# Softmax heads of 128 values kept feature-side, with the probabilities normalised before their turning

## The reference

```python
def _layer_c(x, norm_g, w_in, w_out, pos):
    h = jnp.matmul(_rmsnorm(x, norm_g).astype(x.dtype), w_in)
    cq, ck, cv, z = jnp.split(h, [C_WIDTH, 2 * C_WIDTH, 3 * C_WIDTH], axis=-1)
    yc = _moba_attention(_rope(_heads(cq, C_HEADS), pos), _rope(_heads(ck, C_HEADS), pos), _heads(cv, C_HEADS))
    y = _merge(yc) * jax.nn.silu(z)
    return x + jnp.matmul(y.astype(x.dtype), w_out)
```

## Time and profile before

| | |
|---|---|
| median of 3 runs | 1805.94 us |
| the profiled execution | 1806.85 us |
| its span (first to last instruction) | 1805.0 us |
| TensorE matmuls busy | 1794.4 us, 99% |
| VectorE busy | 1207.6 us, 67% |
| ScalarE busy | 1014.4 us, 56% |
| GpSimd busy | 160.5 us, 9% |
| granted TensorE clock, mean | 0.999 of 2.4 GHz |
| transposes of `ty` (L972) | 112 |
| wide matmuls (L801 to L804) | 768 each |

### The profile page before, as it was taken

The page is one execution under the profiler, slowest core; times in us unless marked ns, Lnnn a source line. Parts: engine busy times, 40 slices in busy tenths (PEclk is TensorE's granted clock), DMA queues, the critical chain, the costliest instruction groups (busy, mean ns, idle before and its releaser), DMA issues.

```text
span 1805.0 us, 26929 instructions
## 1 busy us (share of the span) xinstructions
PE 1794.4 (99%) x10712; PEld 1620.7 (90%) x10712; DVE 1207.6 (67%) x1669; ACT 1014.4 (56%) x1614; POOL 160.5 (9%) x128
## 2 busy tenths in 40 slices
PE   9999999999999999999999999999999999999998
PEld 7999888888899999998889999888888999988887
DVE  6665655555666897697658888655565888855554
ACT  7436546665557765875553444666454344546644
POOL 0000000110011111100001111001000111100101
PEclk9999999999999999999999999999999999999999
DMA  9557555555555555445566555554555655555464
GB/s 361 200 175 223 185 181 191 180 173 189 195 185 170 169 172 174 153 166 173 190 207 203 197 182 187 193 184 166 186 190 197 202 198 175 182 188 185 165 210 139
DMA packets 96620, 340.29 MB, mean 189 GB/s; under 512 B 10880, under 2 KB 11520, under 8 KB 96368
## 3 DMA queue, kind: packets, MB, share of 16 engines
q1 hardware_dynamic: 95120, 334.44, 54.9%
q0 software_dynamic: 944, 3.61, 0.6%
q10 hardware_dynamic: 432, 0.53, 0.1%
HBM read 336.44 MB, written 2.10 MB: 188 GB/s over the span
## 4 chain that ended last, share of the span: by engine, by line
PE 98%; DMA 1%; DVE 0%; ACT 0%; SPq 0%; issue 0%; DVEq 0%; ACTq 0%
PE ACC L796 18%; PE ACC L798 18%; PE ACC L797 18%; PE ACC L804 9%; PE ACC L801 9%; PE ACC L803 5%; PE ACC L802 5%; PE ACC L809 2%; PE ACC L810 2%; PE ACC L811 2%; PE PM L919 1%; PE PM L934 1%; DMA RAW<-in_w 1%; PE PM L972 1%; PE PM L957 1%; PE PM L956 1%
## 5 line engine op out<-in xcount | busy, mean ns | idle before, releaser
L1587 DVE TENSOR_TENSOR WL<-RAW,WH 128x1024 fp32r<-128x1024 f32 (+2 forms) x632 | 792.4, 1271 | 468.6 <-ACT WH L1175 467.2
L1175 ACT ACTIVATE WH<-RAW 128x1024 fp32r<-128x1024 f32 (+3 forms) x633 | 647.2, 1039 | 411.5 <-PE ACC L798 219.1
L796 PE MATMUL ACC<-WH,XHL 128*128 128x512 f32 (+1 forms) x1044 | 395.5, 379 | 0.5 <-DVE WL L1587 0.5
L798 PE MATMUL ACC<-WH,XHL 128*128 128x512 f32 (+1 forms) x1044 | 389.0, 373 | 0.0
L797 PE MATMUL ACC<-WL,XHL 128*128 128x512 f32 (+1 forms) x1044 | 389.0, 373 | 0.0
L801 PE MATMUL ACC<-XHL,WH 128*128 128x512 f32 x768 | 295.6, 385 | 0.0
L804 PE MATMUL ACC<-XHL,WH 128*128 128x512 f32 x768 | 293.4, 382 | 0.0
L796 PEld LDWEIGHTS ACC<-WH,XHL 128*128 128x128 f32 x1044 | 197.4, 189 | 25.5 <-DVE WL L1587 0.9
L798 PEld LDWEIGHTS ACC<-WH,XHL 128*128 128x128 f32 x1044 | 197.3, 189 | 25.5
L797 PEld LDWEIGHTS ACC<-WL,XHL 128*128 128x128 f32 x1044 | 197.4, 189 | 24.4
L803 PE MATMUL ACC<-XHL,WL 128*128 128x256 f32 x768 | 211.2, 275 | 0.0
(11 more groups left out here) (389 smaller groups left out, 2313.0 us busy)
## 6 DMA issues: line engine op xcount, KB each, us to landing
RAW<-in_w SPq DMA_DIRECT2D x605, 512.0 KB, 3.2
RAW<-in_wv SPq DMA_DIRECT2D x24, 344.0 KB, 3.0
X<-in_x SPq DMA_DIRECT2D x4, 512.0 KB, 12.1
RAW<-in_w SPq DMA_DIRECT2D x6, 256.0 KB, 4.5
out<-Y SPq DMA_DIRECT2D x6, 256.0 KB, 3.6
Y<-in_xT SPq DMA_DIRECT2D x2, 512.0 KB, 11.3
S<-in_bias POOLq DMA_DIRECT2D x8, 128.0 KB, 2.3
S<-in_od_gate_w POOLq DMA_DIRECT2D x1, 1024.0 KB, 7.2
```

Of the source, the lines that this page charges most:

```text
L796: e.matmul(o, th, wh, start=f, stop=False)
L798: m = e.matmul(o, tl, wh, start=False, stop=l)
L1175: e.activation(hi, src, ACT.Copy).then_inc(s_hi)
L1587: e.tensor_tensor(lo, src, hi.bitcast(F32), ALU.subtract).then_inc(s_lo)
```

## The change

Softmax heads with 128 values stay feature-side. Their z jobs become `wide` (kind `zT`): VectorE sums the two halves, multiplies by the row of 1/rms (kept in a new buffer ROWZ for layers 2 and 3), and ScalarE applies SiLU in place (`silu_z`). The reciprocal of the sums (`rsum`) is taken off `pT` and stands half a slot behind `scores`, and a new ScalarE step `normal`, one slot behind `scores`, scales the probabilities in two copies; `pT` waits for it. `pv` uses the values as stationary operand and the turned probabilities as moving operand. VectorE multiplies its result by z into Y; for heads 24 to 31, whose z comes later, ScalarE copies it, and GpSimd multiplies later (`gate_z`). `finish` and the turning step of these groups go; `yT` splits Y directly. `load_gain` waits for the last head's product.

```diff
-        both(0, "za", w, 3072, "tok", "silu")
+        wide(0, "za", w, 3072, "zT")
...
-        both(layer, "zs", w, at[1][3], "tok", "silu")
-        both(layer, "zg", w, at[0][3], "tok", "gate")
+        wide(layer, "zs", w, at[1][3], "zT")
+        if layer == 2:
+            both(layer, "zg", w, at[0][3], "tok", "gate")
+        else:
+            wide(layer, "zg", w, at[0][3], "zT")
...
                         put(slot + every * r, step, first + h + (4 if step[0] == "p" else 0), 1)
+                        if step == "scores":
+                            put(slot + every * r + 0.5, "rsum", first + h)
+                            put(slot + every * r + 1, "normal", first + h)
...
             for pair in range(4):
-                put(at + 8 * pair + 13, "finish", (layer, pair))
-                put(at + 8 * pair + 16, "ty", (layer, pair), 1)
-            turn_gated_plan(layer, "zg")
-            if layer == 3:
+                put(L(layer, "zs", pair) + 1, "silu_z", J_OF[layer, "zs", pair])
+                put(at + 8 * pair + 14, "yT", (layer, pair))
+            if layer == 2:
+                turn_gated_plan(layer, "zg")
+            else:
+                for i in range(4):
+                    put(L(3, "zg", i) + 1, "silu_z", J_OF[3, "zg", i])
+                    put(L(3, "zg", i) + 2, "gate_z", i)
+                    put(L(3, "zg", i) + 3, "yT", (3, 4 + i))
...
# TensorE, pT and pv
-                        e.wait_ge(s_ex, 2 * (g - 4) + 2)
+                        e.wait_ge(s_nm, 2 * RC[g - 4])
...
+                if dv == 128:
+                    e.matmul(o[:, 0:256], v[0], p[:, 0:256], start=True, stop=False, skip_group_check=True)
+                    e.matmul(o[:, 128:256], v[1], p[:, 256:384], start=False, stop=True, skip_group_check=True).then_inc(s_pv)
...
# ScalarE
+            def normal(a, _):
+                sc, den = sc_slot(a + 4), cols(a + 4)[:, 2:4]
+                e.wait_ge(s_rc, RC[a])
+                e.activation(sc[:, 0:128], sc[:, 0:128], ACT.Copy, scale=den[:, 0:1]).then_inc(s_nm)
+                e.activation(sc[:, 128:384], sc[:, 128:384], ACT.Copy, scale=den[:, 1:2]).then_inc(s_nm)
+
+            def silu_z(j, _):
+                e.wait_ge(s_evD, D_AT[j])
+                e.activation(z_of(j), z_of(j), ACT.Silu).then_inc(s_zT)
+
+            def yT(item, _):
+                layer, q = item
+                if q > 3:
+                    e.wait_ge(s_gz, q - 3)
+                else:
+                    e.wait_ge(*finished(2 * q + {0: 1, 2: 17, 3: 33}[layer]))
+                e.activation(YH8[q // 4][:, 2 * (q % 4):2 * (q % 4) + 2, :], y_pair(q).rearrange("p (k c) -> p k c", k=2),
+                             ACT.Copy).then_inc(s_yh)
...
+                e.activation(y_of(a), PM[b][:, 0:256], ACT.Copy).then_inc(s_ho)
...
# VectorE
+                elif J.kind == "zT":
+                    e.tensor_reduce(z.rearrange("p g (t c) -> p g t c", t=2), halves_of(j), AX, ALU.add).then_inc(s_evD)
+                    e.wait_ge(s_row, J.layer + 1)
+                    e.wait_ge(s_evD, D_AT[j] - 1)
+                    e.tensor_tensor(z, z, r, ALU.mult).then_inc(s_evD)
...
+                    e.tensor_copy(ROWZ[:, :], PM[b][:, 0:256])
...
+            def rsum(a, _):
+                den = cols(a + 4)[:, 2:4]
+                e.wait_ge(s_ex, 2 * a + 2)
+                e.reciprocal(den, den).then_inc(s_rc)
...
+                e.tensor_tensor(y_of(a), PM[b][:, 0:256], feat(0)[:, h, :], ALU.mult).then_inc(s_yg)
...
# GpSimd
+            def gate_z(i, _):
+                e.wait_ge(s_zT, ZT.index(J_OF[3, "zg", i]) + 1)
+                e.wait_ge(*finished(24 + 2 * i + 1))
+                e.tensor_tensor(y_pair(4 + i), y_pair(4 + i), z_of(J_OF[3, "zg", i]), ALU.mult).then_inc(s_gz)
...
-                e.wait_ge(s_yt, Y_AT[3, 3])
+                e.wait_ge(*finished(39))
```

More of the change, by code:

```diff
@@ L74 @@
 GW, VW3 = 8, 344
-EVAC = {"feat": (0, 2), "few": (0, 1), "copy": (1, 1), "qk": (0, 2), "silu": (2, 0), "gate": (2, 0), "zd": (2, 0),
-        "conv": (2, 0), "sum": (0, 1), "zc": (0, 2), "add": (0, 2), "rope": (0, 4)}
+EVAC = {"feat": (0, 2), "few": (0, 1), "copy": (1, 1), "qk": (0, 2), "gate": (2, 0), "zd": (2, 0),
+        "conv": (2, 0), "sum": (0, 1), "zc": (0, 2), "add": (0, 2), "rope": (0, 4), "zT": (0, 2)}
 BLK = ((0, 0, 0), (128, 1, 0), (256, 1, 1))
@@ L200, in program @@
         YHB, YLB, YHA, YLA = (sb(n, 2048, F32R) for n in ("YHB", "YLB", "YHA", "YLA"))
+        ROWZ = sb("ROWZ", 256)
         S = [S0, S1, S2, S3, S4, S5, S6]
@@ L235, in program @@
         row2 = ROWR.unsqueeze(1).broadcast_to([128, 2, 256])
+        rowz2 = ROWZ[:, :].unsqueeze(1).broadcast_to([128, 2, 256])
         def row_at(layer):
@@ L336, in yc, with y_of, y_pair, z_of @@
             return yC[:, n // 4, n % 4, :]
+        def y_of(a):
+            at, i = 1024 if gated_late(a) else 0, a % 8
+            return Y3[:, i // 4, at + 256 * (i % 4):at + 256 * (i % 4) + 256]
+        def y_pair(q):
+            at = 1024 if q > 3 else 0
+            i = q % 4
+            return Y3[:, i // 2, at + 512 * (i % 2):at + 512 * (i % 2) + 512]
+        def z_of(j):
+            J = jobs[j]
+            return (S6 if J.name == "zg" else S0)[:, 512 * J.b:512 * J.b + 512]
         jobs = job_list()
@@ L355, in program @@
         GATE = [j for j, J in enumerate(jobs) if J.kind == "gate"]
+        ZT = [j for j, J in enumerate(jobs) if J.kind == "zT"]
         ROPE = [j for j, J in enumerate(jobs) if J.kind == "rope"]
@@ L379, in first_of_pair, with gated_late @@
             return is_diff(a) and a % 2 == 0
-        HO = list(accumulate(0 if first_of_pair(a) else 2 for a in range(40)))
+        def gated_late(a):
+            return 24 <= a < 32
+        HO = list(accumulate(2 if is_diff(a) and a % 2 else 1 if gated_late(a) else 0 for a in range(40)))
+        YG = list(accumulate(0 if is_diff(a) or gated_late(a) else 1 for a in range(40)))
         RC = list(accumulate(0 if is_diff(a) else 1 for a in range(40)))
@@ L468, in plan0 @@
             heads_plan(0, at, 4)
-            for slot, pair in ((17, 0), (29, 1), (33, 2), (41, 3)):
-                put(at + slot, "finish", (0, pair))
-                put(at + slot + 3, "ty", (0, pair), 1)
+            for i in range(4):
+                put(L(0, "za", i) + 1, "silu_z", J_OF[0, "za", i])
+            for slot, pair in ((18, 0), (30, 1), (34, 2), (42, 3)):
+                put(at + slot, "yT", (0, pair))
             turn_gated_plan(0, "zb")
@@ L570, in program @@
                 plan[slot][n] = (step, item, got[0] if wants == 1 else got)
+                if step in ("ty", "yT"):
+                    Y_AT[item] = len(Y_AT) + 1
                 if step == "ty":
-                    Y_AT[item] = len(Y_AT) + 1
-                if step == "finish":
-                    FIN_AT[item] = len(FIN_AT) + 1
+                    T_AT[item] = len(T_AT) + 1
                 if step == "few":
@@ L961, in ty @@
                 layer, q = item
[L962 to L965, removed]
+                if layer == 1:
                     e.wait_ge(s_gd1, 4 * (q - 3))
@@ L1198, in evacuate @@
                                          accum_out=sums[:, t, 4 * J.b + h:4 * J.b + h + 1]).then_inc(s_qsq)
[L1199 to L1206, removed]
                 elif J.kind == "gate":
@@ L1346, in pv @@
             def pv(g, b):
-                a, den = g - 4, cols(g)[:, 2:4]
-                if g < 4:
+                a = g - 4
+                if not is_diff(a) and not gated_late(a):
                     return
@@ L1533, in scalar @@
                      "decay_rows": decay_rows, "cols": columns_step, "rows": rows, "decay": decay, "pT": pT,
-                     "norm_qk": norm_qk, "qkT": qkT, "scores": scores, "mix1": mix1, "pv": pv, "ty": ty, "copied": copied, "silu": silu, "decays1": decays1,
+                     "norm_qk": norm_qk, "qkT": qkT, "scores": scores, "normal": normal, "silu_z": silu_z, "yT": yT, "mix1": mix1, "pv": pv, "ty": ty, "copied": copied, "silu": silu, "decays1": decays1,
                      "decays2": decays2, "norm_sq": norm_sq, "norm_sum": norm_sum, "turn_v": turn_v, "delta_a": delta_a, "tri": tri, "small_x": small_x,
@@ L1598, in evacuate @@
                     e.tensor_tensor(f, f, row2, ALU.mult).then_inc(s_evD)
+                elif J.kind == "zT":
+                    z, r = two(z_of(j)), rowz2 if J.layer else row2
+                    e.wait_ge(s_mm, p + 1)
+                    if J.name == "zg":
+                        e.wait_ge(s_rot, len(ROPE))
+                        e.wait_ge(s_gm, 2 * len(GATE))
+                    elif J.layer == 0:
+                        e.wait_ge(s_msc, 4)
+                    else:
+                        e.wait_ge(s_sc, 16 if J.layer == 2 else 32)
+                    e.tensor_reduce(z.rearrange("p g (t c) -> p g t c", t=2), halves_of(j), AX, ALU.add).then_inc(s_evD)
+                    e.wait_ge(s_row, J.layer + 1)
```

(18 more changed lines are left out.)

32 lines of the change are left out of this document (11 added, 21 removed).

## The result

The changed kernel takes 1816.6 us (median of 6 runs, 1815.4 to 1817.0), the kernel before 1806.2 us in the same comparison: a ratio of 1.0056, with an interval of 1.0045 to 1.0066. The forecast was 1809.0 us with a range up to 1814. The profiled execution took 1816.64 us for a span of 1814.6 us, 9.6 us longer than before.

A forecast was written before the change was run, and what follows sets the result against it. The prediction took TensorE, streaming almost without waits, as the bound, with VectorE pacing itself in layer 3's rope stage. Columns -5.5 us plus a stall of 8.5 us gave +3.0 us on 1805.94: 1809.0 us, range 1802 to 1814.

The forecast's parts named there:

- Columns: TensorE's work over the run: its columns change by -5.5 us in all.
- the three terms: TensorE: turning steps removed -7.0 us, token-side jobs made wide +2.0 us, values as weights -0.5 us.
- The hand-over: Layer 3, heads 24 to 31: VectorE's split waits behind ScalarE's scalings, 1.98 us a round; TensorE stands still 8.5 us.
- The second half of layer 3: Heads 32 to 39: VectorE 6.1 us late against 5.7 us of pT slack, just level: 0, bounds 0 and +5.
- both halves: Rival, chance 0.18: layer 3's second-half rounds take 13.6 us, pT of heads 36 to 39 waits, 4.8 us more: 1813.8 us.

The follow-up runs named there:

- n2_all: The changed kernel with the scalings of all 32 heads one slot later (two slots behind scores): 1801.7 us, ratio 0.9973 to the kernel before.
- before_hand: The kernel before with only reciprocals half a slot and scalings one slot behind scores, z, values and turning steps kept: 1815.1 us, ratio 1.0048.
- first4: The changed kernel with the scalings one slot later for all heads but 24 to 27: 1804.9 us, ratio 0.9991 to the kernel before.
- out_by_four: n2_rope with layer 3's first two output jobs alternating by four pieces and not by two: 1810.5 us, ratio 1.0025 to the kernel before.
- acc_early: n2_rope with TensorE's wait for a z job's accumulator asking for the reduction alone, not the product behind it: 1806.2 us, ratio 0.9999.
- n2_late: The changed kernel with the scalings one slot later for heads 32 to 39 alone: 1810.4 us, ratio 1.0023 to the kernel before.
- n2_rope: The changed kernel with the scalings one slot later for heads 24 to 31 alone: 1807.3 us, ratio 1.0005 to the kernel before.

## Why the prediction was wrong

*Columns: right.* Forecast -5.5 us. The changed kernel without its waits (n2_all) is 4.7 us under the kernel before (2.9 to 6.7 by its interval), so the three terms are right in sum; no run has them one by one. Its span is 5.1 us shorter, but the profiled execution of the kernel before was 0.9 us above its median. Transposes of the turning step fell to 48 and the wide lines rose to 1024 each, as forecast.

*The hand-over: right, with its size.* Forecast: 1.98 us in a round, a round of 13.95 us, no wait before head 27, then 1.2 and four times 1.8 us, 8.5 us in all. Measured: 1.98, 13.95, none before head 27, then 1.2 and four times 1.8 (distances of 13.33 and 13.95 us against 12.12), 8.5 us. before_hand shows it by itself, 8.7 us; first4 shows that it adds up.

*The second half of layer 3: the step that failed.* The working put VectorE 6.1 us late at head 39 and compared this with one thing alone, the 5.7 us of slack of `pT`; it put the stage at 0. The lateness was somewhat too large: VectorE's mask of head 39 is at 1715.74 and `pT` at 1721.54, 5.8 us, where n2_all has 10.87 us (1702.35 to 1713.22), so it is 5.1 us. The 5.8 us are more than the 5.1 us that the chain from the mask to the end of the scalings needs (to 1720.81), and `pT` does not wait. So on `pT` the working was right. But another consumer of VectorE's lateness has less slack, the accumulator. The working had looked at it in the rope stage only ("the job that needs its accumulator starts 6.2 us behind them") and says nothing of it for the second half. In the rope stage the next job but one starts four pieces behind a wide job's end. Behind the last z job it starts two pieces behind, because the first two output jobs alternate by two pieces, as `piece_list` says. The z evacuation's own place in the round (from 7.2 us to 9.2 us behind the mask) was in the text. In n2_all, where VectorE is not late, the last z product leaves this slack (timelines of VectorE and TensorE):

```profile
1702.35 0.56 DVE L1835 SCALAR_TENSOR_TENSOR SC<-PM,C 128x384 f32<-128x384 f32 x1 [0.34 <-PE PM L954]
...
1709.72 0.69 DVE L1657 TENSOR_TENSOR S<-S,ROWZ 128x512 f32<-128x512 f32 x1
...
1713.46 0.46 PE L831 MATMUL ACC<-WH,YHB 128*128 128x512 f32 x1
```

The product ends at 1710.41 and the output job starts at 1713.46: 3.05 us of slack, about half of `pT`'s. In the changed kernel the product comes 6.7 us later against TensorE: 5.1 us from the rounds before and 1.7 us from the hand-over in its own round (it starts 9.04 us behind the mask and not 7.37). 6.7 - 3.05 = 3.7 us, against a measured wait of 3.6. That it is this accumulator is what out_by_four and acc_early show.

*The clock: a term that was missing.* The working has no price for what a longer wait does to the clock. No wait of the kernel before was long enough to show it. Its trace has the fall only behind TensorE's last matmul, which ends at 1797.2, and there it costs nothing (columns as in the stretches above):

```profile
1798.00:1800.00 2.00, 0.00 (x0) 0.00 (x0) 1.59 (x5) 1.54 (x4) 0.00 (x0) 1.00 0.28 91
1800.00:1805.00 5.00, 0.00 (x0) 0.00 (x0) 0.70 (x2) 0.14 (x1) 0.00 (x0) 0.52 0.62 210
```

Behind the wait of 3.6 us the granted clock fell, and 2.6 us more were lost. That size is read from the distances of the matmuls; no run has the wait without the half clock. n2_late, which has neither, is 6.2 us under the changed kernel.

The account by spans: 1799.9 (n2_all) + 8.5 + 3.6 + 2.6 = 1814.6 us, the measured span. That it meets the tenth is luck, since the spans of one kernel's executions differ by 1 to 3 us. The forecast lacked the last two terms, 6.2 us, and had them partly in the rival "both halves" (1813.8 us), which had the right stage and the wrong consumer. It also wanted rounds of 13.6 us, and the seven rounds between the masks of heads 32 and 39 take 12.75 us on average (1626.50 to 1715.74). The bounds of that stage, 0 and +5 us, were too narrow for the same reason.

The Trainium skill ("ScalarE: Activation LUTs", section "What ACT_TABLE_LOAD costs") has a drain of about 1.38 us with each table load, by which the z rounds would be longer. The trace doesn't agree: in the kernel before, the evacuation of a z job starts at 1710.92, right at the end of its load (1709.62 + 1.28), as in the earlier trace rows. n2_late and n2_all have the same loads as the changed kernel and no second wait.

## What to carry to other kernels

Where two in-order engines hand each piece to one another, a step that needs a fresh result from the other engine should not stand in front of a hand-over which that engine waits for. One slot of place was worth 15 us here (1816.6 and 1801.7 us), and the work itself nothing that could be measured. When an engine's round is longer than that of the bound one, multiply the difference by the rounds and compare it with the slack of every consumer of its results and not with the first one found. Accumulators and buffers belong to these, in their real order at the stage's end. And look for such a chain where an engine waits only for its partner and never for the bound engine: there the slack is not shown by its busy share.

## What was not expected of the hardware

Stretches at half clock followed the four longest waits that were traced. Each is one execution (us, then busy us of PE, PEld, DVE, ACT, POOL, PEclk, DMA share, GB/s); n2_rope and then out_by_four:

```profile
1718.10:1721.40 3.30, 3.30 (x9) 2.58 (x9) 3.30 (x3) 3.18 (x5) 2.13 (x1) 0.50 0.02 5
```

```profile
1721.80:1728.50 6.70, 5.43 (x13) 4.37 (x14) 2.26 (x3) 0.00 (x0) 0.00 (x0) 0.50 0.01 2
```

| run | wait of TensorE | at half clock |
|---|---|---|
| changed kernel | 3.6 us | 6.8 us |
| n2_rope | 3.6 us | 3.4 us |
| acc_early | 2.8 us | 3.4 us |
| out_by_four | 6.6 us | 6.8 us |

Waits of up to 1.7 us, five in a row with 12 us of work between them, were followed by none. So the length of the wait alone doesn't give the length of the stretch: 3.6 us were followed once by 6.8 us and once by 3.4 us. In the changed kernel and in out_by_four the clock fell while TensorE was still idle (at 1724.0, and the matmuls start again at 1725.6; at 1721.7 and 1723.1), in n2_rope and acc_early just after they had started again (at 1718.0 and 1717.0; starts at 1717.9 and 1716.7). The first two had the long stretch, the last two the short one. Four executions don't show why.
